# One set of squares, weighted two ways: the double norm behind a feed-forward loop

## The chip, the cores and the metric

One core of one Trainium2 chip runs the whole program. The metric is device microseconds of one execution, median of the runs. TensorE is PE in the rows (PEld its weight loads), VectorE is DVE, ScalarE is ACT, SyncE is SP; GpSimd (POOL) has six instructions and plays no part here.

## The reference, cut to what matters

Two transformer blocks follow each other on 256 tokens of width 1024, all in float32. The first block ends in a feed-forward layer and a final norm; the second begins with a norm of its own and a projection. So two norms stand in a row, with no matmul between them:

```
h = h + _swiglu(_rmsnorm(h, norm_ffn_w), w_gate, w_up, w_down)   # first block
x = _rmsnorm(h, norm_final_w)[:, N_META:]                        # final norm, gain g
...
u = _rmsnorm_2(x, mix_norm_g_2[0])                               # second block, gain m
p = u @ ev_w_in_2                                                # sq, sk, za, sv parts of p
...
x = x + _even_mixer(...)                                         # x itself is needed again
```

With S1 = sum of h² and S2 = sum of (g h)² over the 1024 features, the final norm's factor is rf = 1/sqrt(S1/D + eps), and the second norm's factor on top is 1/sqrt(rf² S2/D + eps). The product of both is 1/sqrt(sum of (g² + eps) h² / D + eps²): one weighted sum, one root, one reciprocal. The factor rf alone is still needed for x, which the residual adds later.

## The kernel before

Tokens lie along the free axis (256 columns), features along the partitions (8 tiles of 128, index k). Every weight matrix streams through in chunks of 2048 columns a partition, in a ring of four slots. SP loads a chunk (`raw`), ACT rounds it (`whi`, L1035), DVE takes the rest (`wlo`, L1409), and PE multiplies with three matmuls a tile (L417: high by high, high by low, low by high). This rounding and subtracting is called splitting a chunk here. A slot's next load waits for the split, and ACT's next rounding in a slot for PE's last use of it.

ACT and DVE split by `pump(n)`, called from their own program: it splits all chunks up to n + 3 that are not split yet, so a chunk's split stands in each engine's queue at a fixed place, behind whatever is written ahead of it. Each engine runs its instructions strictly in the written order; semaphores join them. The order is written out by hand.

PE's projections use `proj`, two pairs of PSUM banks by turns: a projection begins when the chunk is split (`lo_ready`) and when DVE has read out the chunk two before (`proj_free`).

Around the change, in order of the program:

- The feed-forward loop ends. For each of four pairs of feature tiles DVE adds the result to `x_all` (semaphore `x_new`), ACT rounds two tiles to `u` (L1190) and squares the pair (L1191, into region f2), and DVE takes the low part of `u` (L1412, `u_ready`). In the kernel before ACT then squares both tiles again with the final gain as scale (L1196, into f3), and only then posts `sq_ready`.
- PE projects chunk sq0. In its first half a gate ahead of every second tile waits for `u_ready`, and sums the squares of the pair before by matmuls with a matrix of ones (`square_pair`, L474 plain and L479 with the gain).
- ACT takes the root of the plain sum (L1044); DVE makes rf (L1785), turns the second sum into a mean, ACT takes its root (L1254), DVE inverts (L1789) and multiplies: `rms`, the combined factor.
- DVE reads out sq0, sq1, sk0, sk1 with `rms`, and behind sq0 and sq1 scales four tiles each of `x_all` by rf (`x_all` L1412). PE projects sq1, sk0, sk1, turns `rms` into a column for each token (L488), transposes eight small tiles (L811), projects za2, sums squares of q and k for their own norms (L820), projects za3, spreads the factors (L827), projects za0, and the attention begins.

Of the kernel before, what the change touches and what calls it, by code (L numbers as in the profile page):

```python
# [7 lines left out]
ALU = mybir.AluOpType  # L8
ACT = mybir.ActivationFunctionType
# [175 lines left out]
def build(nc, w, params, consts, late, ln_gb, out):  # L185
# [11 lines left out]
    with ExitStack() as ctx:  # L197
# [21 lines left out]
        def C(name):  # L219
            a, n = CONST_COLS[name]  # L220
            return cst[:, a:a + n]
# [43 lines left out]
        both_gains = small[:, 64:72]  # L265

# [140 lines left out]
        def _(pe):  # L407
# [62 lines left out]
            def square_pair(c, norm_no, tokens=S, second=False):  # L470

                pe.wait_ge(sems["sq_ready"], 4 * norm_no + c + 1)
                for k in (2 * c, 2 * c + 1):
                    ins = mm(aux[:, 0, 0:tokens], C("ones"), sq_of(tokens)[:, k, :], start=k == 0, stop=k == KT - 1,  # L474
                             skip_group_check=True)
                if second and c:

                    for k in range(0 if c == 1 else 2 * c, 2 * c + 2):
                        ins = mm(aux[:, 1, 0:S], C("ones"), f("f3", 0, KT, S)[:, k, :], start=k == 0, stop=k == KT - 1,  # L479
                                 skip_group_check=True)  # L480
                if c == 3:
                    ins.then_inc(sems["sumsq"], 1)

# [7 lines left out]
            def sq_of(tokens):  # L491
                return sq if tokens == L else f("f2", 0, KT, S)
# [312 lines left out]
            for name in ("sq1", "sk0", "sk1"):  # L805
                project(name, t0=META, t=S)
            turn_norm(2)
# [216 lines left out]
        def _(eng):  # L1024
# [154 lines left out]
            def norm(source, gain, norm_no, second=False):  # L1179

                for c in range(4):
                    if isinstance(source, str):

                        pump(index[f"{source}{min(c + 1, 3)}"])
                        read_out(f"{source}{c}")
                    else:
                        eng.wait_ge(sems["x_new"], 4 * source + c + 1)
                    pair = x2[:, 2 * c:2 * c + 2, :]
                    for k in (2 * c, 2 * c + 1):
                        A.post(act(u[:, 0, k, META:L], x2[:, k, :], ACT.Copy, scale=gain(k)), "u_hi")  # L1190
                    ins = act(f("f2", 0, KT, S)[:, 2 * c:2 * c + 2, :], pair, ACT.Square)  # L1191
                    if second:
                        A.run(ins)

                        for k in (2 * c, 2 * c + 1):
                            ins = act(f("f3", 0, KT, S)[:, k, :], x2[:, k, :], ACT.Square, scale=V("final", k))  # L1196
                            if k % 2 == 0:
                                A.run(ins)
                    A.post(ins, "sq_ready")
                if not isinstance(source, str):  # L1200

                    pump(loop_last[source] - 1)
                eng.wait_ge(sems["sumsq"], norm_no + 1)
                root(aux[:, 0, 0:S], r_all[:, 0, 0:S], 1.0 / D, eps, "root_ready")
# [46 lines left out]
            norm(0, lambda k: both_gains[:, k:k + 1], 2, second=True)  # L1251

            eng.wait_ge(sems["second_mean"], 1)
            A.post(act(r_all[:, 2, 0:S], r_all[:, 2, 0:S], ACT.Sqrt, bias=eps, scale=1.0 / D), "second_root")  # L1254
# [147 lines left out]
        def _(eng):  # L1402
# [41 lines left out]
            B.run(ve.memset(eps, EPS))  # L1444
            B.run(ve.memset(gn_eps, GN_EPS))
# [39 lines left out]
            for k in range(4, KT):  # L1485
                keep(k)
            B.run(tt(both_gains, par[:, PAR_COLS["final"][0]:PAR_COLS["final"][0] + KT],
                     par[:, PAR_COLS["mix2"][0]:PAR_COLS["mix2"][0] + KT], ALU.mult))
            pump(index["rq0"] - AHEAD + 2)
# [293 lines left out]
            rf, rm = r_all[:, 1, 0:S], r_all[:, 2, 0:S]  # L1783
            eng.wait_ge(sems["root_ready"], 5)
            B.run(ve.reciprocal(rf, rms))  # L1785
            B.run(tt(rm, rf, rf, ALU.mult))
            B.post(tt(rm, rm, aux[:, 1, 0:S], ALU.mult), "second_mean")
            eng.wait_ge(sems["second_root"], 1)
            B.run(ve.reciprocal(rm, rm))  # L1789
            B.post(tt(rms, rf, rm, ALU.mult), "rms_ready")  # L1790
# [4 lines left out]
            for j, name in enumerate(("sq", "sk")):  # L1795
                for c in range(2):
                    b = arrive(f"{name}{c}", urgent=j == c == 0)
                    freed(tt(pre[j][:, 2 * c:2 * c + 2, :], proj[:, b:b + 2, 0:S], bc(rms, 2), ALU.mult))
                    if j == 0:

                        for k in range(4 * c, 4 * c + 4):
                            B.run(stt(x2[:, k, :], x2[:, k, :], V("final", k), rf, ALU.mult, ALU.mult))
# [8 lines left out]
            token_factors(1)  # L1811
            eng.wait_ge(sems["late_in"], 16)
# [8 lines left out]
            B.run(ve.tensor_copy(ident_r, C("ident")))  # L1821
            B.run(ts(mask_r, LC("mask_strict")[:, 0:P], 1.0, ALU.subtract, MASKED, ALU.mult))
            za_part(2)

            B.run(ve.tensor_copy(f("f5", 0, 16, 64)[0:16], C("ident")[0:16, 0:16][:, :, None].to_broadcast([16, 16, 64])))
# [315 lines left out]
```

## Time and profile before

| | |
|---|---|
| median of 3 runs | 1178.59 us (1178.41 to 1178.78) |
| profiled execution, its own time | 1178.25 us |
| its span, first to last instruction | 1176.5 us |
| mean granted TensorE clock | 0.977 |
| PE busy | 1122.0 us (95%), 8656 matmuls |
| DVE busy | 745.9 us (63%), 813 instructions |
| ACT busy | 508.6 us (43%), 506 instructions |
| DMA | 177.63 MB, mean 151 GB/s |

The time stands 1.75 us above the span: start and end of the program lie outside it. A busy PE is the rule here, so the places to read are those at which PE waits. A clock of 1.00 is TensorE's 2.4 GHz level, 0.50 its 1.2 GHz level. One matmul in float32 leaves two entries in the trace, one in the rounded type one.

### The profile page before, as it was taken

Reading aid. Unit: us, or ns where it says so; the run is one execution under the profiler, and the core shown is the slowest. Engines: PE = TensorE matmul, PEld = TensorE weight load, DVE = VectorE, ACT = ScalarE, POOL = GpSimd, SP = SyncE. Lnnn points to the kernel's source line nnn. Section 1 sums busy time; section 2 is a strip of 40 time slices with the busy share of each in tenths; the row PEclk is TensorE's granted clock in tenths of the full one; section 3 lists DMA queues with packets and bytes.
Section 4 is the critical chain, followed back from the end, with each engine's and each line's share of the span. In section 5 each row is a group of like instructions: output and inputs, shape, how many; then the busy total and the mean of one; then the engine's idle time right before and its main releaser. Section 6 shows DMA issues by size and latency. Waiting matters only on the chain.

```text
span 1176.5 us, 21013 instructions
## 1 busy us (share of the span) xinstructions
PE 1122.0 (95%) x8656; PEld 1068.6 (91%) x8656; DVE 745.9 (63%) x813; ACT 508.6 (43%) x506; POOL 6.0 (1%) x6
## 2 busy tenths in 40 slices
PE   8999998899999999998998999999988999999998
PEld 7998885788989999988887999999978999999998
DVE  5764747576756666668746565555479776655563
ACT  5523332433544444455484444333443455434331
POOL 0000001000000000000000000000000000000000
PEclk8999999899999999999999999999898999999999
DMA  9673243134427565664423464654253435564630
GB/s 299 188 211 108 90 143 108 44 130 154 129 72 210 166 203 170 191 201 150 150 95 108 143 215 158 199 177 145 85 165 112 139 108 176 183 211 157 203 107 36
DMA packets 162590, 177.63 MB, mean 151 GB/s; under 512 B 4800, under 2 KB 148288, under 8 KB 162536
## 3 DMA queue, kind: packets, MB, share of 16 engines
q1 hardware_dynamic: 160704, 174.56, 46.9%
q10 hardware_dynamic: 1832, 2.30, 1.0%
q8 instruction: 40, 0.66, 0.2%
q14 instruction: 14, 0.11, 0.0%
HBM read 175.27 MB, written 1.57 MB: 150 GB/s over the span
## 4 chain that ended last, share of the span: by engine, by line
PE 79%; DVE 12%; ACT 5%; issue 2%; DMA 2%; ACTq 0%; SPq 0%; DVEq 0%
PE proj L417 48%; PE aux L778 20%; DVE wlo L1409 4%; DVE f L1412 2%; DVE f L1409 2%; PE aux L474 2%; ACT whi L1035 1%; PE aux L705 1%; DMA gamma_rows<-f 1%; DVE f L1415 1%; PE aux L688 1%; PE aux L585 1%; PE aux L574 1%; DMA f<-in_x_dram 1%; PE aux L698 1%
## 5 line engine op out<-in xcount | busy, mean ns | idle before, releaser
L417 PE MATMUL proj<-u,whi 128*128 128x256 f32 (+1 forms) x2912 | 538.7, 286 | 11.2 <-DVE wlo L1409 4.1
L1409 DVE TENSOR_TENSOR wlo<-raw,whi 128x2048 fp32r<-128x2048 f32 (+2 forms) x176 | 374.2, 2126 | 159.7 <-ACT whi L1035 151.7
L417 PEld LDWEIGHTS proj<-u,whi 128*128 128x128 f32 x2912 | 455.9, 191 | 20.3 <-issue 8.0
L417 PE MATMUL proj<-u,wlo 128*128 128x256 f32 (+1 forms) x1456 | 413.7, 284 | 0.0
L1035 ACT ACTIVATE whi<-raw 128x2048 fp32r<-128x2048 f32 (+3 forms) x174 | 311.6, 1791 | 124.8 <-PE proj L417 56.0
L417 PEld LDWEIGHTS proj<-u,wlo 128*128 128x128 f32 x1456 | 279.0, 192 | 0.0
L778 PE MATMUL aux<-v,whi 128*128 128x256 f32 x1376 | 249.9, 283 | 2.7 <-DVE v L1409 2.5
L778 PEld LDWEIGHTS aux<-v,whi 128*128 128x128 f32 x1376 | 214.2, 192 | 3.4 <-issue 3.4
L778 PE MATMUL aux<-v,wlo 128*128 128x256 f32 x688 | 194.6, 283 | 0.0
L778 PEld LDWEIGHTS aux<-v,wlo 128*128 128x128 f32 x688 | 131.9, 192 | 0.0
L417 PE MATMUL proj<-v,whi 128*128 128x256 f32 (+2 forms) x592 | 109.1, 286 | 6.5 <-DVE f L1409 3.4
L417 PEld LDWEIGHTS proj<-v,whi 128*128 128x128 f32 (+1 forms) x592 | 91.5, 189 | 10.6 <-issue 5.8
L1234 ACT ACTIVATE v<-f 128x512 fp32r<-128x512 f32 x32 | 20.2, 631 | 165.0 <-DVE f L1409 165.0
L417 PE MATMUL proj<-v,wlo 128*128 128x256 f32 (+2 forms) x296 | 83.7, 283 | 0.0
L417 PE MATMUL proj<-whi,u 128*128 128x256 f32 (+1 forms) x352 | 68.9, 290 | 4.1 <-DVE f L1415 2.5
L1409 DVE TENSOR_TENSOR f<-proj,r_all 128x256 f32<-128x256 f32 (+6 forms) x89 | 50.2, 564 | 27.4 <-PE proj L417 23.4
L417 PEld LDWEIGHTS proj<-whi,u 128*128 128x128 f32 x352 | 58.2, 199 | 5.9 <-issue 4.2
L417 PEld LDWEIGHTS proj<-v,wlo 128*128 128x128 f32 (+1 forms) x296 | 55.9, 189 | 0.0
L1409 DVE TENSOR_TENSOR v<-f,v 128x512 fp32r<-128x512 f32 (+1 forms) x54 | 31.5, 584 | 38.0 <-ACT v L1234 24.7
L417 PE MATMUL proj<-wlo,u 128*128 128x256 f32 (+1 forms) x176 | 50.8, 289 | 0.0
L1412 DVE SCALAR_TENSOR_TENSOR f<-proj,r_all 128x512 f32<-128x512 f32 x32 | 22.1, 692 | 44.1 <-PE proj L417 43.5
L1409 DVE TENSOR_TENSOR f<-f 128x512 f32<-128x512 f32 (+5 forms) x63 | 40.7, 646 | 2.2
(263 smaller groups left out, 752.3 us busy)
## 6 DMA issues: line engine op xcount, KB each, us to landing
raw<-in_mlp_w_dram SPq DMA_DIRECT2D x64, 1024.0 KB, 5.3
raw<-in_w_in_dram SPq DMA_DIRECT2D x21, 1024.0 KB, 6.9
raw<-in_od_w_in_dram SPq DMA_DIRECT2D x12, 1024.0 KB, 5.4
raw<-in_w_ffn_gate_dram SPq DMA_DIRECT2D x22, 512.0 KB, 3.9
raw<-in_w_ffn_up_dram SPq DMA_DIRECT2D x22, 512.0 KB, 5.2
raw<-in_w_ffn_down_dram SPq DMA_DIRECT2D x21, 512.0 KB, 5.3
raw<-in_ev_w_in_dram SPq DMA_DIRECT2D x10, 1024.0 KB, 5.6
raw<-in_w_ret_out_dram SPq DMA_DIRECT2D x4, 1024.0 KB, 5.3
```

Of the source, the lines that this page charges most:

```text
L417: ins = mm(o, w_of(a, k), x_of(b, k), start=first and k == 0 and j == 0, stop=last and k == kt - 1 and j == 2, skip_group_check=skip)
L474: ins = mm(aux[:, 0, 0:tokens], C("ones"), sq_of(tokens)[:, k, :], start=k == 0, stop=k == KT - 1, skip_group_check=True)
L574: ins = mm(aux[:, 2 * (h % 2), j * S:(j + 1) * S], k_ret[p0:p0 + 64, h // 2, t:t + P], q_ret[p0:p0 + 64, h // 2, :], start=True, stop=True)
L585: ins = mm(o, rv_tok[:, 1 - j, h * P:(h + 1) * P], sd[:, h % 2, j, :], start=False, stop=j == 1)
L688: ins = mm(aux[:, b, 0:L], q_all[0:96, h, b * P:(b + 1) * P], k_all[0:96, h, :], start=True, stop=True)
L698: ins = nc.tensor.transpose(o, prob[:, h % 2, b, t:t + m], C("ident"))
L705: ins = mm(aux[p0:p0 + 64, 3, S:2 * S], v_tok[0:m, j, 64 * h:64 * h + 64], pt[0:m, j, :], start=j == 0, stop=j == 2)
L778: ins = mm(aux[:, j // 2, (j % 2) * S:(j % 2 + 1) * S], W(a, n, 0, kt, D)[:, q, j * P:(j + 1) * P], v[:, b, 2 * (k % 2) + q, :], start=fir ...
L1035: A.post(act(whi[:, n % RING, 0:wd], raw[:, n % RING, 0:wd], ACT.Copy), "hi_ready")
L1234: A.post(act(v[:, 0, 2 * (k % 2):2 * (k % 2) + 2, :], f("f1", 512, 2, S), ACT.Copy), "hidden_hi")
L1409: return ve.tensor_tensor(o, a, b, op)
L1412: return ve.scalar_tensor_tensor(out=o, in0=a, scalar=s, in1=b, op0=op0, op1=op1)
```

## The change

ACT no longer squares a second time. The one set of squares is summed twice: first with weights g² + eps (a column of eight values for each partition, spread over 128 columns by an address step of zero), inside the gate of sq0, and then with ones, in `first_sums` behind sq0. The first sum gives the combined factor by one root (bias eps²) and one reciprocal; the second gives rf by one root and one reciprocal. The weights are made once near the program's start. The scaling of `x_all` by rf is put behind later read-outs, and three small preparations on DVE (two casts or copies of an identity, one mask) come earlier.

```diff
@@ PE
                 for k in (2 * c, 2 * c + 1):
-                    ins = mm(aux[:, 0, 0:tokens], C("ones"), sq_of(tokens)[:, k, :], start=k == 0, stop=k == KT - 1,
+                    weights = gains_and_eps[:, k:k + 1].to_broadcast([P, P]) if second else C("ones")
+                    ins = mm(aux[:, 0, 0:tokens], weights, sq_of(tokens)[:, k, :], start=k == 0, stop=k == KT - 1,
                              skip_group_check=True)
-                if second and c:
-                    for k in range(0 if c == 1 else 2 * c, 2 * c + 2):
-                        ins = mm(aux[:, 1, 0:S], C("ones"), f("f3", 0, KT, S)[:, k, :], start=k == 0, stop=k == KT - 1,
-                                 skip_group_check=True)
+            def first_sums():
+                for k in range(KT):
+                    ins = mm(aux[:, 1, 0:S], C("ones"), sq_of(S)[:, k, :], start=k == 0, stop=k == KT - 1)
+                ins.then_inc(sems["first_sums"], 1)
...
             project("sq0", t0=META, t=S, gate=by_pair(2, second=True))
-            for name in ("sq1", "sk0", "sk1"):
+            first_sums()
+            project("sq1", t0=META, t=S)
+            turn_norm(2)
+            for name in ("sk0", "sk1"):
                 project(name, t0=META, t=S)
-            turn_norm(2)
@@ ACT
-                    if second:
-                        A.run(ins)
-                        for k in (2 * c, 2 * c + 1):
-                            ins = act(f("f3", 0, KT, S)[:, k, :], x2[:, k, :], ACT.Square, scale=V("final", k))
-                            if k % 2 == 0:
-                                A.run(ins)
...
-            eng.wait_ge(sems["second_mean"], 1)
-            A.post(act(r_all[:, 2, 0:S], r_all[:, 2, 0:S], ACT.Sqrt, bias=eps, scale=1.0 / D), "second_root")
+            eng.wait_ge(sems["first_sums"], 1)
+            root(aux[:, 1, 0:S], r_all[:, 1, 0:S], 1.0 / D, eps, "first_root")
@@ DVE
+            B.run(ve.memset(eps_sq, EPS * EPS))
...
+            B.run(tt(gains_and_eps, final_gains, final_gains, ALU.mult))
+            B.run(ts(gains_and_eps, gains_and_eps, EPS, ALU.add))
...
-            eng.wait_ge(sems["root_ready"], 5)
-            B.run(ve.reciprocal(rf, rms))
-            B.run(tt(rm, rf, rf, ALU.mult))
-            B.post(tt(rm, rm, aux[:, 1, 0:S], ALU.mult), "second_mean")
-            eng.wait_ge(sems["second_root"], 1)
-            B.run(ve.reciprocal(rm, rm))
-            B.post(tt(rms, rf, rm, ALU.mult), "rms_ready")
+            norm_scale(2)
...
+            qk_raw(0, 0, urgent=True)
+            eng.wait_ge(sems["late_in"], 16)
+            B.run(ve.tensor_copy(f("f5", 0, 16, 64)[0:16], C("ident")[0:16, 0:16][:, :, None].to_broadcast([16, 16, 64])))
+            B.run(ve.tensor_copy(ident_r, C("ident")))
+            B.run(ts(mask_r, LC("mask_strict")[:, 0:P], 1.0, ALU.subtract, MASKED, ALU.mult))
+            qk_raw(0, 1)
+            eng.wait_ge(sems["first_root"], 1)
+            B.run(ve.reciprocal(rf, rf))
+            final_scale(0, 2)
+            qk_raw(1, 0)
+            token_factors(1)
+            final_scale(2, 6)
+            qk_raw(1, 1)
...
             za_part(2)
+            final_scale(6, 8)
```

Here `qk_raw(j, c)` is the read-out of sq0, sq1, sk0, sk1 in turn (with the splits that its `arrive` pumps; the first pumps none), and `final_scale` the scaling of `x_all` by rf.

**PE, the gate of sq0.** Names: `aux` is the PSUM tensor of the sums, f2 and f3 the regions of squares, cst the ones, small the new weights. Before, from the second pair of tiles on:

```order
L474 MATMUL aux<-f2,cst 128x256 [waits sq_ready]
L474 MATMUL aux<-f2,cst 128x256
L479 MATMUL aux<-f3,cst 128x256 x4
L417 MATMUL proj<-u,whi 128x256 [waits u_ready]
...
L474 MATMUL aux<-f2,cst 128x256 [waits sq_ready]
L474 MATMUL aux<-f2,cst 128x256
L479 MATMUL aux<-f3,cst 128x256 x2
L474 MATMUL aux<-f2,cst 128x256 [waits sq_ready]
L474 MATMUL aux<-f2,cst 128x256
L479 MATMUL aux<-f3,cst 128x256 x2
```

and after the change, with the place behind sq0:

```order
L476 MATMUL aux<-f2,small 128x256 [waits sq_ready]
L476 MATMUL aux<-f2,small 128x256
L418 MATMUL proj<-u,whi 128x256 [waits u_ready]
...
L476 MATMUL aux<-f2,small 128x256 [waits sq_ready]
L476 MATMUL aux<-f2,small 128x256
L476 MATMUL aux<-f2,small 128x256 [waits sq_ready]
L476 MATMUL aux<-f2,small 128x256
...
L484 MATMUL aux<-f2,cst 128x256 x8
L418 MATMUL proj<-u,whi 128x256 [waits proj_free,lo_ready]
```

The eight matmuls of the second sum have moved from between the gate's waits to a place between sq0 and sq1, and take the plain squares.

**ACT, behind the last squares.** `raw`, `whi` are a chunk's slots; the three roundings are those of sk0, sk1 and za2. Before, then after:

```order
L1035 ACTIVATE whi<-raw 128x2048 [waits chunk_used,raw_landed1,sq_ready]
L1044 ACT_TABLE_LOAD [waits sumsq]
L1044 ACTIVATE r_all<-aux,small 128x256 [waits hi_ready]
L1254 ACTIVATE r_all<-r_all,small 128x256 [waits second_mean,root_ready]
L1035 ACTIVATE whi<-raw 128x2048 [waits chunk_used,raw_landed2,second_root]
```

```order
L1040 ACTIVATE whi<-raw 128x2048 [waits chunk_used,raw_landed1,sq_ready]
L1049 ACT_TABLE_LOAD [waits sumsq]
L1049 ACTIVATE r_all<-aux,small 128x256 [waits hi_ready]
L1049 ACTIVATE r_all<-aux,small 128x256 [waits first_sums,root_ready]
L1040 ACTIVATE whi<-raw 128x2048 [waits chunk_used,raw_landed2,first_root]
```

The second root now waits for PE's `first_sums`, where it waited for DVE's mean, and the rounding of sk0 still stands behind it.

**DVE, from the factor to the read-out of sq1.** Before (the three `wlo` are the splits of sk0, sk1, za2), then after:

```order
L1785 RECIPROCAL r_all<-r_all 128x256 [waits root_ready,lo_ready]
L1409 TENSOR_TENSOR r_all<-r_all 128x256 [waits dve_step]
L1409 TENSOR_TENSOR r_all<-r_all,aux 128x256 [waits dve_step]
L1789 RECIPROCAL r_all<-r_all 128x256 [waits second_root,second_mean]
L1409 TENSOR_TENSOR r_all<-r_all 128x256 [waits dve_step]
L1415 TENSOR_SCALAR small<-par 128x1 [waits rms_ready]
L1409 TENSOR_TENSOR f1<-proj,r_all 128x512 [waits chunk_used,dve_step]
L1412 SCALAR_TENSOR_TENSOR x_all<-x_all,par,r_all 128x256 [waits proj_free]
L1412 SCALAR_TENSOR_TENSOR x_all<-x_all,par,r_all 128x256 [waits dve_step] x3
L1409 TENSOR_TENSOR wlo<-raw,whi 128x2048 [waits hi_ready,dve_step]
L1409 TENSOR_TENSOR wlo<-raw,whi 128x2048 [waits hi_ready,lo_ready] x2
L1409 TENSOR_TENSOR f1<-proj,r_all 128x512 [waits chunk_used,lo_ready]
```

```order
L1717 RECIPROCAL r_all<-r_all 128x256 [waits root_ready,lo_ready]
L1412 TENSOR_SCALAR small<-par 128x1 [waits rms_ready]
L1406 TENSOR_TENSOR f1<-proj,r_all 128x512 [waits chunk_used,dve_step]
L1800 COPY f5<-cst 16x1024 [waits late_in,proj_free]
L1801 CAST v<-cst 128x128 [waits dve_step]
L1412 TENSOR_SCALAR v<-cst 128x128 [waits dve_step]
L1406 TENSOR_TENSOR wlo<-raw,whi 128x2048 [waits hi_ready,dve_step]
L1406 TENSOR_TENSOR wlo<-raw,whi 128x2048 [waits hi_ready,lo_ready] x2
L1406 TENSOR_TENSOR f1<-proj,r_all 128x512 [waits chunk_used,lo_ready]
L1805 RECIPROCAL r_all<-r_all 128x256 [waits first_root,proj_free]
L1409 SCALAR_TENSOR_TENSOR x_all<-x_all,par,r_all 128x256 [waits dve_step] x2
L1406 TENSOR_TENSOR wlo<-raw,whi 128x2048 [waits hi_ready,dve_step]
```

Ahead of the split of sk0 one reciprocal, three products and four scalings are gone, and three small preparations have come; the reciprocal for rf and two scalings now stand behind the read-out of sq1.

## Rows read from the trace of the kernel before

**Rows 1.** The page, chain that ended last: shares of the span by engine.
```profile
PE 79%; DVE 12%; ACT 5%; issue 2%; DMA 2%; ACTq 0%; SPq 0%; DVEq 0%
```
**Rows 2.** The chain in order of time, 505 to 600 us: start, us, what.
```profile
518.55 0.70 DVE x_all L1409
...
519.34 0.52 ACT u L1190
...
520.42 0.64 ACT f L1191
521.08 0.52 ACT f L1196
...
530.65 1.92 ACT whi L1035
...
532.66 2.30 DVE wlo L1409
534.98 1.76 DVE r_all L1785
...
538.36 1.76 DVE r_all L1789
...
541.52 0.50 DVE x_all L1412
...
543.61 2.30 DVE wlo L1409
545.95 13.12 PE proj L417 x96
559.07 0.53 PE aux L488 x4
559.60 1.02 PE aux L811 x8
560.62 5.68 PE proj L417 x48
...
575.75 3.65 PE aux L827 x16
579.39 7.39 PE proj L417 x48
```
**Rows 3.** Groups of ACT's instructions, 519 to 531 us.
```profile
L1196 ACT ACTIVATE f<-x_all,par 128x256 f32<-128x256 f32 x8 | 4.1, 509 | 0.3
```
**Rows 4.** Stretches: length, then busy us of each engine, PEclk, DMA share, GB/s.
```profile
520.40:533.00 12.60, 10.85 (x57) 8.75 (x56) 5.19 (x11) 11.81 (x20) 0.00 (x0) 1.00 0.01 2
...
541.90:545.90 4.00, 0.00 (x0) 0.00 (x0) 3.85 (x5) 2.16 (x2) 0.00 (x0) 1.00 0.00 0
546.10:549.40 3.30, 3.30 (x16) 3.30 (x17) 3.27 (x2) 0.00 (x0) 0.00 (x0) 0.50 0.69 228
...
580.10:583.60 3.50, 3.50 (x19) 3.50 (x18) 3.33 (x6) 1.35 (x2) 0.00 (x0) 0.51 0.00 0
```
**Rows 5.** PE in order of time, the first matmul of sq0 and its restart.
```profile
521.15 0.35 PE L417 MATMUL proj<-u,whi 128*128 128x256 f32 x1 [0.55 <-DVE u L1412]
...
532.31 0.47 PE L417 MATMUL proj<-u,whi 128*128 128x256 f32 x1
```
**Rows 6.** The chain later, two float32 sums (four entries) of a plain norm.
```profile
654.04 0.86 PE aux L474 x4
```
**Rows 7.** Line 670, weight loads with an address step of zero: min/median/max ns.
```profile
L670 PEld LDWEIGHTS aux<-f,cst x16: 180/185/185, 196.3 to 199.5; 8*128 8x128 f32 x16
```
**Rows 8.** ACT in order of time, the squares of q.
```profile
551.36 1.06 ACT L1259 ACTIVATE f<-f 128x1024 f32<-128x1024 f32 x1 [7.27 <-DVE f L1409]
```
**Rows 9.** DVE in order of time, near the program's start and at 567 us.
```profile
20.12 0.17 DVE L1409 TENSOR_TENSOR small<-par 128x8 f32<-128x8 f32 x1
...
23.45 2.29 DVE L1409 TENSOR_TENSOR wlo<-raw,whi 128x2048 fp32r<-128x2048 f32 x1 [0.84 <-ACT whi L1035]
...
567.46 0.68 DVE L1825 COPY f<-cst 16x1024 f32<-16x1024 f32 x1
```

More of the change, by code:

```diff
@@ L265, in build @@
         both_gains = small[:, 64:72]
+        gains_and_eps, eps_sq = small[:, 8:16], small[:, 3:4]
         x_tok = f("f1", 0, 3, D)
@@ L1177, in _, with norm @@
                 A.post(act(v[:, 0, 2 * j:2 * j + 2, :], yr[:, 2 * j:2 * j + 2], ACT.Copy, scale=0.5), "merged_hi")
-            def norm(source, gain, norm_no, second=False):
+            def norm(source, gain, norm_no, eps_ap=eps):
                 for c in range(4):
@@ L1203, in norm @@
                 eng.wait_ge(sems["sumsq"], norm_no + 1)
-                root(aux[:, 0, 0:S], r_all[:, 0, 0:S], 1.0 / D, eps, "root_ready")
+                root(aux[:, 0, 0:S], r_all[:, 0, 0:S], 1.0 / D, eps_ap, "root_ready")
             def hidden_layer(d):
@@ L1250, in _ @@
             hidden_layer(FFN)
-            norm(0, lambda k: both_gains[:, k:k + 1], 2, second=True)
-            eng.wait_ge(sems["second_mean"], 1)
-            A.post(act(r_all[:, 2, 0:S], r_all[:, 2, 0:S], ACT.Sqrt, bias=eps, scale=1.0 / D), "second_root")
+            norm(0, lambda k: both_gains[:, k:k + 1], 2, eps_ap=eps_sq)
+            eng.wait_ge(sems["first_sums"], 1)
+            root(aux[:, 1, 0:S], r_all[:, 1, 0:S], 1.0 / D, eps, "first_root")
             for j, name in enumerate(("sq", "sk")):
@@ L1488, in _ @@
                      par[:, PAR_COLS["mix2"][0]:PAR_COLS["mix2"][0] + KT], ALU.mult))
+            final_gains = par[:, PAR_COLS["final"][0]:PAR_COLS["final"][0] + KT]
+            B.run(tt(gains_and_eps, final_gains, final_gains, ALU.mult))
+            B.run(ts(gains_and_eps, gains_and_eps, EPS, ALU.add))
             pump(index["rq0"] - AHEAD + 2)
@@ L1780, in _ @@
             hidden_layer(FFN, 0, lambda k: both_gains[:, k:k + 1], 2)
-            rf, rm = r_all[:, 1, 0:S], r_all[:, 2, 0:S]
-            eng.wait_ge(sems["root_ready"], 5)
-            B.run(ve.reciprocal(rf, rms))
-            B.run(tt(rm, rf, rf, ALU.mult))
-            B.post(tt(rm, rm, aux[:, 1, 0:S], ALU.mult), "second_mean")
-            eng.wait_ge(sems["second_root"], 1)
-            B.run(ve.reciprocal(rm, rm))
-            B.post(tt(rms, rf, rm, ALU.mult), "rms_ready")
+            rf = r_all[:, 1, 0:S]
+            norm_scale(2)
             pre = (f("f1", 0, 4, S), f("f1", 1024, 4, S))
@@ L1794, in _, with qk_raw, final_scale @@
             B.run(ts(qg8, V("sb_q"), 0.125, ALU.mult))
[L1795 to L1802, printed above, removed]
+            def qk_raw(j, c, urgent=False):
+                b = arrive(f"{'sq' if j == 0 else 'sk'}{c}", urgent=urgent)
+                freed(tt(pre[j][:, 2 * c:2 * c + 2, :], proj[:, b:b + 2, 0:S], bc(rms, 2), ALU.mult))
+            def final_scale(k0, k1):
+                for k in range(k0, k1):
+                    B.run(stt(x2[:, k, :], x2[:, k, :], V("final", k), rf, ALU.mult, ALU.mult))
+            qk_raw(0, 0, urgent=True)
[11 more added lines that the diff above has]
+            qk_raw(1, 1)
             def per_token(name, dst, width=256):
@@ L1809, in per_token @@
                 freed(ins)
-            token_factors(1)
-            eng.wait_ge(sems["late_in"], 16)
             eng.wait_ge(sems["sg_turned"], 1)
@@ L1819, in za_part @@
                 per_token(f"za{a}", lambda j: za[:, j, a * 256:(a + 1) * 256])
-            B.run(ve.tensor_copy(ident_r, C("ident")))
-            B.run(ts(mask_r, LC("mask_strict")[:, 0:P], 1.0, ALU.subtract, MASKED, ALU.mult))
             za_part(2)
-            B.run(ve.tensor_copy(f("f5", 0, 16, 64)[0:16], C("ident")[0:16, 0:16][:, :, None].to_broadcast([16, 16, 64])))
+            final_scale(6, 8)
             eng.wait_ge(sems["sb_root"], 1)
```

## The prediction, made before the changed kernel ran

> **What bounds the kernel now.** I read the chain that ended last first: PE holds 79% of the span, DVE 12%, ACT 5% [rows 1]. So the time is PE's row of work plus the places where PE waits, and the change can only pay at such a place. The chain in order of time shows one between 518 and 560 us [rows 2]: it leaves PE for ACT at 519.34 and stays with ACT, over four pairs of tiles, until 530.65, goes through ACT's rounding and DVE's split of sq1, then through DVE's reciprocals, its scaling of `x_all` and the split of sk0, and comes back to PE at 545.95. The second squares stand in it: eight instructions of 256 columns, 509 ns each, 4.1 us in all [rows 3]. The stretches show what PE did meanwhile: busy 10.85 of 12.60 us in the gate, nothing at all from 541.90 to 545.90, and then 3.30 us of work at a granted clock of 0.50, the 1.2 GHz level [rows 4].
>
> **The change on PE's row, step by step.** I count from sq0's first matmul (521.15) to the eight transposes L811 (559.60), which is 38.45 us [rows 2, 5].
>
> *The gate.* From 521.15 to sq0's restart at 532.31 are 11.16 us [rows 5]. The work in it is 18 matmuls of the rounded type at 0.118 (5.68 us for 48 [rows 2]), 2.1 us, and 16 float32 sums, 32 entries at 0.215 (0.86 for four [rows 6]), 6.9 us: 9.0, so PE waited 2.15. After the change a pair costs ACT two roundings and one square, 519.34 to 521.08, or 1.74 us [rows 2], so the four pairs last until 526.3 where they lasted until 530.65. DVE's pace per pair, one addition of 0.70 and two low parts of about 0.5 (bounded by the 0.50 of a scaling with the same 256 columns [rows 2]), is about 1.75 with gaps: the two engines run level, and DVE cannot make it worse by more than about 0.1. The last two sums, 0.86, follow the last square, so sq0 restarts at about 527.25. That is 6.1 us for 2.1 + 3.45 of work: waits of 0.55. **Gain 1.6.** The other eight sums, 3.45 us, are not saved: they move behind sq0.
>
> *The wait for sk0.* Before, PE stands idle 4.05 us (541.90 to 545.95 [rows 2, 4]) for the split of sk0, which stands on DVE behind two reciprocals of 1.76, three products, and four scalings of 0.50 [rows 2]. After: sq0 ends 30 matmuls (3.55) after 527.25, at 530.8, the first sums at 534.25 (call it T). The root waits there, ACT needs about 0.5 for it (256 columns, as its rounding of 0.52) and 1.92 for sk0, DVE 2.30 for the split [rows 2]: with 0.3 for handing over, sk0 is split at T + 5.1. PE meanwhile does sq1 (5.7) and L488 (0.53), until T + 6.2. The idle time is gone, with 1.1 us to spare. **Gain 4.05.**
>
> *The half-rate stretch.* sk0 and sk1 took 13.12 us where 96 matmuls at full clock take 2 x 5.68 = 11.36 [rows 2]; the clock fell as PE's idle time ended [rows 4]. Without the idle time there is no reason for it. **Gain 1.75.**
>
> Here a rule of the Trainium skill speaks against the change. In this case's rows the gate, 12.60 us with 1.75 of it idle in several short pieces, ran at 1.00 throughout [rows 4], so shorter waits in it should cost nothing. TensorE: Matmul & The Clock Gate, section "A second HAM failure mode: psum-queue depth-cycling", says that frequent short idle times between groups of matmuls make the clock swing between its two levels. If it held in the new gate, one stretch at half rate would come back, priced like the old one, and the sum would be 5.65 in place of 7.4. The trace disagrees for the old gate, which had more waiting in it, so I keep the row's answer.
>
> *Costs.* The weights with an address step of zero: the trace has such loads, 8 partitions by 128 columns, at 185 ns [rows 7]; a load below the 0.215 us between entries lies beside the matmuls. I take nothing for them; the bound below is nothing (a shorter load is hidden as well), the bound above is in the rivals. The setup on DVE, a product of 8 columns (0.17 [rows 9]) and an addition of the same size, about 0.4 with gaps, and a memset that is smaller still, stands ahead of a split that waited 0.84 for ACT behind it [rows 9]: nothing. Without that cover it would be 0.4. The three preparations on DVE, 0.68 [rows 9] and two of 128 columns that I bound by 0.5 each, at most 1.7, run between the read-out of sq0 (about 533.3) and the rounding of sk0 (T + 2.7 = 537.0), where DVE has 3.7 us to wait. Without that cover they would cost up to 1.7 less the 1.1 to spare.
>
> *What is late next.* All of ACT's and DVE's work up to the attention's norms hangs on T too, so I put both queues beside PE's, in us after T, with 2.30 a split, 1.92 a rounding, 0.70 a read-out (as the addition of 512 columns), 1.76 a reciprocal, 0.50 a scaling [rows 2]. PE wants sk0 at 6.2, sk1 at 11.9, za2 at 18.6 (after L811's 1.02), L820 at 24.3. DVE ends the splits of sk1 and za2 at 9.7 and reads out sq1 at 10.4, which frees sk1's banks: 1.5 to spare. The reciprocal for rf, two scalings, the split of za3 and the read-out of sk0 end at 16.5: 2.1 to spare for za2. Four scalings, the split of za0 and the read-out of sk1 end at 21.9, ACT's squares (1.06 [rows 8]) at 23.0: 1.3 to spare for L820. So nothing overtakes PE, but no cover is above 2.1. From L827 on (575.75 before) everything in the chain is released by PE and moves with it.
>
> **Sum.** 1.6 + 4.05 + 1.75 = 7.4 us. The profiled execution's 1178.25 (span 1176.5 plus 1.75 outside) becomes 1170.85; the median of the runs lies 0.34 higher, so 1171.2.
>
> **Rivals.**
>
> *The clock gives back more (chance 0.15).* At 580.10 to 583.60 PE ran at 0.51 with no idle time ahead of it, right behind L827's 3.65 us of small matmuls; za0 took 7.39 instead of 5.68 [rows 2, 4]. That stretch is not tied to a wait of PE. If it does not come back at its new place, 1.7 more is gained: 1169.5. Against it: the four times of the kernel before lie within 0.53 us, so its half-rate stretches hardly wander. By the Trainium skill, TensorE: Matmul & The Clock Gate, Part 1, the monitor runs free of the kernel's start, so where a stretch falls may change from run to run; by that rule the times would scatter by such amounts. No run here shows that they do.
>
> *A wait takes the old one's place (0.20).* ACT now stands at `first_sums` with the roundings of sk0, sk1, za2 behind it, and DVE's splits behind those. If these queues are slower than I add up, by more than the 1.1 to 1.5 us of cover, PE waits again at sk0, at sk1 or at L820. Each us beyond costs one; an idle time as long as the old one would bring the half-rate stretch with it. With 1 to 2.5 us late, and the stretch (1.75) or not, the gain is 3 to 6.4: 1172.2 to 1175.6. For it: four covers must hold at once. Against: they come from measured durations and all start at one point.
>
> *The gain is taken back later (0.05).* If the attention after 586 us were held by something that does not move with PE, the time would be about 1178. Against: the chain enters it through PE [rows 2].
>
> *Slow weights (0.05, slower in 0.03).* The sixteen loads of 128 partitions with a step of zero have no row; the nearest has 8 partitions [rows 7]. Beyond 0.215 us each costs its excess. The whole gain of 7.4 is gone at 0.215 + 7.4/16 = 0.68 us a load, 3.7 times the row; at 1.0 us the cost is 12.6 and the time 1183.8. Against: a step of zero took no longer than a common load there.
>
> **How the numbers follow.** My forecast has 0.55, with a range of its own of 1170.0 to 1172.2 (0.2 for DVE's pace and setup, 0.7 for handing over, both ways). The predicted time is its 1171.2. The range for 8 in 10 reaches down to the first rival less its spread, 1168.9, and up through most of the second, 1174.5. About 0.2%, 2.4 us, is what a measurement of this kernel can tell from no change. Faster by more: 0.55 + 0.15 + 0.20 = 0.90. Within: 0.05 + 0.02 = 0.07. Slower: 0.03.
>
> **What would show it right or wrong.** ACT's four pairs end near 526.3 and `first_sums` near 534.3. PE shows no idle time over 1 us between 527 and 560 and a clock of 1.00 there. L811 begins near 552.2 and L827 near 568.3. The new sums' entries stand 0.215 apart; if they are further apart, the weights are slow. If PE waits before sk0, sk1 or L820, the row ahead of it names the cover that failed. If L811 comes at 552 and the end still does not move by 7, the chain behind 586 us was wrong.

## The result, and the profile after

| | before | changed |
|---|---|---|
| median us (runs) | 1178.59 (7: 1173.00 to 1179.25) | 1168.09 (7: 1167.41 to 1169.47) |
| profiled execution: time, span us | 1178.25, 1176.5 | 1167.41, 1165.6 |
| mean granted clock | 0.977 | 0.978 |
| PE busy | 1122.0 us, 95% | 1118.1 us, 96% |

The ratio is 0.9921 [0.9907, 0.9935]: the change is worth 9.3 us of 1178.59 (7.7 to 11.0). The forecast of 1171.2 had the sign; its gain of 7.4 us falls 1.9 short of that. The median lies 3.1 us below the forecast and 0.8 us below the lower end of the range; the ratio times 1178.59, 1169.3, lies within it.

The page's shares of the chain that ended last have moved from DVE to PE, against [rows 1]:

```profile
PE 80%; DVE 10%; ACT 5%; issue 2%; DMA 2%; ACTq 0%; SPq 0%; DVEq 0%
```

The chain of the changed kernel in order of time (start, us, what) answers to [rows 2]. L476 are the weighted sums in the gate, L484 `first_sums`, L491 the turning of the factor, L816 the eight transposes, L825 the sums of q and k, L832 the spreads (L827 before), L845 the first scores.

```profile
520.08 0.94 PE proj L418 x6
521.02 0.86 PE aux L476 x4
521.88 0.84 PE proj L418 x6
...
524.48 1.92 PE aux L476 x8
526.40 3.51 PE proj L418 x30
529.92 3.46 PE aux L484 x16
533.37 5.64 PE proj L418 x48
539.01 0.53 PE aux L491 x4
539.54 11.56 PE proj L418 x96
551.10 0.88 PE aux L816 x8
...
557.65 3.56 PE aux L825 x16
...
567.08 3.65 PE aux L832 x16
570.73 5.88 PE proj L418 x48
576.61 0.64 PE aux L845 x4
```

From 520.08 to 576.61 the chain stays with PE: in the chain before it left for ACT at 519.34 and came back at 545.95. The gate takes 6.32 us (520.08 to 526.40), sq1 follows `first_sums` at once, and 96 matmuls of sk0 and sk1 take 11.56 where they took 13.12. From sq0's first matmul to the transposes are 31.02 us, 38.45 before: **7.43 less**. Below I give this stretch by the starts in PE's own order of time, which go a little differently about the transposes: 38.38 before, 30.86 after, 7.52 less.

The same engine by stretches (length, then busy us of PE, weight loads, DVE, ACT, POOL, then PEclk, DMA share, GB/s) answers to [rows 4]. PE is busy for the whole gate, and where it stood still from 541.90 on it now runs at 1.00. Behind the spreads no half rate shows either: za0's 48 matmuls take 5.88 in the chain above, where they took 7.39.

```profile
520.40:533.00 12.60, 12.60 (x80) 11.01 (x79) 9.42 (x13) 8.24 (x12) 0.00 (x0) 1.00 0.18 59
533.00:541.90 8.90, 8.90 (x74) 8.73 (x73) 6.29 (x5) 6.22 (x4) 0.00 (x0) 1.00 0.38 126
541.90:552.00 10.10, 10.10 (x88) 10.10 (x87) 9.37 (x12) 4.90 (x3) 0.00 (x0) 1.00 0.90 283
```

ACT and DVE in order of time (start, us, instruction, in brackets the idle time ahead of it and who ended it):

```profile
525.25 1.91 ACT L1040 ACTIVATE whi<-raw 128x2048 fp32r<-128x2048 f32 x1
...
533.47 0.47 ACT L1049 ACTIVATE r_all<-aux,small 128x256 f32<-128x256 f32 x1 [4.52 <-PE aux L484]
...
536.00 6.94 DVE L1406 TENSOR_TENSOR wlo<-raw,whi 128x2048 fp32r<-128x2048 f32 x3 [2.50 <-ACT whi L1040]
542.98 0.69 DVE L1406 TENSOR_TENSOR f<-proj,r_all 128x512 f32<-128x512 f32 x1
...
549.20 0.69 DVE L1406 TENSOR_TENSOR f<-proj,r_all 128x512 f32<-128x512 f32 x1
...
554.52 0.69 DVE L1406 TENSOR_TENSOR f<-proj,r_all 128x512 f32<-128x512 f32 x1
555.31 1.06 ACT L1256 ACTIVATE f<-f 128x1024 f32<-128x1024 f32 x1 [6.58 <-DVE f L1406]
```

ACT ends its pairs at 525.22, does the rounding of sq1 and the first root, and then waits 4.52 us for `first_sums`; DVE's split of sk0 is the first of the three at 536.00 and ends at 536.00 + 2.30 = 538.3, while PE wants it at 539.54. So the wait has changed sides: ACT and DVE wait for PE.

### The profile page after: what moved, and what is told of

It reads as the page before. It is cut to its first block, busy times and chain, and to the rows that moved or that the text cites. A ratio compares the mean times of both kernels' runs of the same rounds, so it can differ in the third digit from the quotient of the medians.

```text
span 1165.6 us, 21006 instructions
## 1 busy us (share of the span) xinstructions
PE 1118.1 (96%) x8656; PEld 1063.9 (91%) x8656; DVE 745.0 (64%) x813; ACT 504.6 (43%) x498; POOL 6.0 (1%) x6
## 4 chain that ended last, share of the span: by engine, by line
PE 80%; DVE 10%; ACT 5%; issue 2%; DMA 2%; ACTq 0%; SPq 0%; DVEq 0%
PE proj L418 49%; PE aux L781 20%; DVE wlo L1406 4%; DVE f L1409 2%; DVE f L1406 2%; PE aux L476 2%; ACT whi L1040 1%; PE aux L708 1%; DMA gamma_rows<-f 1%; PE aux L691 1%; DVE f L1412 1%; PE aux L588 1%; PE aux L577 1%; PE aux L701 1%; DMA f<-in_x_dram 0%
## 5 line engine op out<-in xcount | busy, mean ns | idle before, releaser
L418 PE MATMUL proj<-whi,u 128*128 128x256 f32 (+1 forms) x352 | 66.4, 284 | 4.0 <-DVE f L1412 2.5
```

Source lines behind the costliest of these rows:

```text
L418: ins = mm(o, w_of(a, k), x_of(b, k), start=first and k == 0 and j == 0, stop=last and k == kt - 1 and j == 2, skip_group_check=skip)
```

## The experiments

The theory to be tested: PE's row is the bound, and the gain is the second squares (gate, and the chain to sk0 behind it), the idle time ahead of sk0, and the half-rate stretch that this idle time brought. The rival: other edits (the order of the scalings, the place of the sums) or only the clock did it. "Stretch" is from sq0's first matmul to the first transpose in the profile; "spreads to scores" is from L827 or L832 to the first scores, 9.5 us where PE has the full clock and 11.0 with one half-rate stretch. Both columns are of the one profiled execution of a run. Times are medians of all its executions; each ratio is against the kernel before, run beside it (its medians there: 1177.39, 1176.26, 1176.90).

| run | median us | ratio | stretch | spreads to scores |
|---|---|---|---|---|
| before (first profile) | 1178.59 | 1 | 38.38 | 11.04 |
| changed (first profile) | 1168.09 | 0.9921 [0.9907, 0.9935] | 30.86 | 9.53 |
| e1_squares_back | 1172.90 | 0.9968 [0.9955, 0.9982] | 35.18 | 11.03 |
| e2_scalings_only | 1172.49 | 0.9967 [0.9956, 0.9978] | 36.31 | 9.52 |
| e3_norm_only | 1169.83 | 0.9943 [0.9927, 0.9959] | 31.64 | 11.04 |
| e4_pe_filled | 1176.23 | 0.9995 [0.9982, 1.0008] | 36.87 | 12.62 |
| e5_sums_in_gate | 1166.60 | 0.9925 [0.9901, 0.9950] | 30.51 | 9.53 |
| e6_rounded_sums | 1165.74 | 0.9911 [0.9892, 0.9930] | 27.70 | 9.52 |
| after_again (the changed kernel) | 1168.65 | 0.9931 [0.9908, 0.9953] | 30.93 | 9.52 |
| before_again (the kernel before) | 1176.65 | 1.0002 [0.9987, 1.0016] | 38.37 | 11.03 |
| e7_rounded_in_gate | 1165.22 | 0.9906 [0.9888, 0.9924] | 27.39 | 12.63 |
| after_third | 1168.40 | 0.9940 [0.9920, 0.9959] | 30.91 | 9.52 |
| before_third | 1176.78 | 1.0005 [0.9988, 1.0022] | 38.42 | 11.02 |

**The second squares back on ACT.** The changed kernel, but ACT squares each pair a second time; nobody reads these squares.

```diff
                     ins = act(f("f2", 0, KT, S)[:, 2 * c:2 * c + 2, :], pair, ACT.Square)
+                    if second:
+                        A.run(ins)
+                        for k in (2 * c, 2 * c + 1):
+                            ins = act(f("f3", 0, KT, S)[:, k, :], x2[:, k, :], ACT.Square, scale=V("final", k))
...
                     A.post(ins, "sq_ready")
```

> The changed kernel, with ACT's eight second squares put back ahead of each sq_ready (written to their old region, read by nobody). The measure is the stretch from sq0's first matmul to the first of the eight transposes: 38.45 us before, 31.02 in the changed kernel. Theory (three waits of PE: the gate 1.6, the wait for sk0 4.05, the half-rate stretch 1.75): ACT's four pairs last 4.3 us longer, PE waits for them in the gate, sq0 restarts some 10.3 us after its first matmul in place of 6.3, and nothing else changes, since all later queues start at the end of the first sums: stretch 35.0, some 4 us above the changed kernel. Rival (the squares were hidden, the gain is DVE's shorter path to the split of sk0): stretch 31 to 31.5.

The chain of this kernel:

```profile
528.62 0.52 ACT f L1200
...
530.31 3.51 PE proj L418 x30
...
543.45 11.56 PE proj L418 x96
...
570.99 3.79 PE aux L832 x16
574.78 7.24 PE proj L418 x48
```

ACT paces the gate again: sq0 restarts 10.64 us after its first matmul (519.67) instead of 6.32, and all the rest of the stretch is as in the changed kernel, down to the 11.56 of sk0 and sk1. The squares cost 35.18 - 30.86 = 4.3 us, eight times 0.54, as the theory had it. The gate as a stretch:

```profile
519.70:531.00 11.30, 8.07 (x42) 5.99 (x43) 4.14 (x8) 10.75 (x18) 0.00 (x0) 1.00 0.00 1
```

PE waits 3.2 us of it, in several pieces, at 1.00. But the half-rate stretch behind the spreads is there (7.24 for za0's 48 matmuls), although the sums and the norm are the new ones.

**The order of the scalings alone.** The kernel before, with its two sets of squares and its norm; only the scaling of `x_all` stands where the change puts it.

```diff
...
+            qk_raw(0, 0, urgent=True)
+            qk_raw(0, 1)
+            final_scale(0, 2)
+            qk_raw(1, 0)
+            final_scale(2, 6)
+            qk_raw(1, 1)
...
             za_part(2)
-
+            final_scale(6, 8)
```

> The kernel before, with one part of the change: the scalings of x_all by rf are moved behind later read-outs, none is left ahead of the split of sk0. Norm, squares and sums stay as before. Theory: the split of sk0 comes four scalings, 2.05 us, earlier, so PE's idle time of 4.07 us shrinks to about 2.0; if that is too short for the clock to fall, the half-rate stretch goes too: measured stretch 38.45 - 2.05 - 1.75 = 34.65; if the clock still falls, 36.4. Rival (the moved scalings matter little, the norm's own path is all): stretch 38 or more.

PE in order of time at sk0, and a stretch of the same kernel:

```profile
541.98 0.50 PE L417 MATMUL proj<-u,whi 128*128 128x256 f32 x2 [1.98 <-DVE wlo L1409]
```

```profile
543.20:546.50 3.30, 3.30 (x17) 3.30 (x17) 3.27 (x2) 0.00 (x0) 0.00 (x0) 0.50 1.00 339
```

The idle time at sk0 is 1.98 in place of 4.05, so the stretch is 2.07 shorter: four scalings of 0.50. The clock fell all the same, as PE's work came back: half the idle time saved only itself. Without the half-rate stretch 34.65 was expected. Behind the spreads this kernel, with the old norm, shows none. Its time fell by more than the stretch, 2.6 to 5.2 us for 2.07: as in the changed kernel, part of what was gained lies outside the stretch.

**The norm alone.** The changed kernel with the scalings, the three preparations and the factors at the places where the kernel before has them.

```diff
             qk_raw(0, 0, urgent=True)
...
             eng.wait_ge(sems["first_root"], 1)
             B.run(ve.reciprocal(rf, rf))
-            final_scale(0, 2)
+            final_scale(0, 4)
+            qk_raw(0, 1)
+            final_scale(4, 8)
             qk_raw(1, 0)
...
```

> The changed kernel with the other part undone: the scalings of x_all are back behind the read-outs of sq0 and sq1, four and four, and the three preparations back at their old places; the norm with one set of squares stays. Theory: DVE does the reciprocal for rf and four scalings, 3.9 us, before the split of sk0, starting when the first root is there (0.8 us behind the end of the first sums), so that split ends about 7.0 us behind them where PE wants it at 6.2: PE waits some 0.8 us, stretch 31.8, and the clock stays at 1.00. Rival (the order on DVE is worth a large part of the gain): stretch 33 or more.

The chain of this kernel at sk0,

```profile
538.59 2.30 DVE wlo L1406
...
540.93 11.61 PE proj L418 x96
```

and PE in order of time at the same place:

```profile
540.93 0.50 PE L418 MATMUL proj<-u,whi 128*128 128x256 f32 x2 [0.69 <-DVE wlo L1406]
```

The reciprocal and four scalings stand ahead of the split again, the cover of 1.1 us is used up, and PE waits 0.69 for it; the clock stayed up (11.61). So the order is worth 0.8 us (31.64 - 30.86) on top of the norm and 2.07 without it: the norm carries 6.7 of the 7.5. The two do not add up, because both take away from the one wait.

**PE filled.** The kernel before with 32 unused matmuls between sq1 and sk0, so that PE has work while it waits.

```diff
-            for name in ("sq1", "sk0", "sk1"):
+            project("sq1", t0=META, t=S)
+            for j in range(32):
+                mm(aux[:, 3, 0:S], u[:, 0, j % KT, META:META + P], u[:, 1, j % KT, META:L], start=True, stop=True)
+            for name in ("sk0", "sk1"):
...
```

> The kernel before with 32 more matmuls on PE behind sq1, into a bank that nobody reads, of the rounded type with 256 columns: 32 x 0.118 = 3.8 us of work in the place of the 4.07 us in which PE stood idle for the split of sk0. All waits stay. Theory (idle time alone makes the clock fall there): sk0 and sk1 take about 11.4 us in place of 13.12, the stretch shrinks by 1.75 to 36.7 though PE does more. Rival (the clock falls there for another reason): sk0 and sk1 still take about 13, stretch 38.4.

PE in order of time, and the chain of this kernel:

```profile
539.73 3.95 PE L807 MATMUL aux<-u 128*128 128x256 f32 x32
543.94 0.51 PE L417 MATMUL proj<-u,whi 128*128 128x256 f32 x2 [0.26 <-DVE wlo L1412]
```

```profile
543.94 11.62 PE proj L417 x96
...
572.23 4.85 PE aux L830 x16
577.09 7.77 PE proj L417 x48
```

sk0 begins as late as ever, but sk0 and sk1 take 11.62 instead of 13.12: the idle time did bring the half rate, and it cost 1.5 us. The time does not show it: the ratio's interval, 0.9982 to 1.0008, holds 1.5 us as well as nothing. In the profiled execution the last two rows say where it went: the half-rate stretch behind the spreads is twice as long, 12.62 us from spreads to scores where the kernel before has 11.04. There the clock took back 30 us later what it had given at sk0.

**The plain sums inside the gate.** The changed kernel with the matmuls of `first_sums` behind each pair's weighted sums, where the kernel before had its second sums.

```diff
+                if second and c:
+                    for k in range(0 if c == 1 else 2 * c, 2 * c + 2):
+                        ins = mm(aux[:, 1, 0:S], C("ones"), sq_of(S)[:, k, :], start=k == 0, stop=k == KT - 1,
...
-            first_sums()
             project("sq1", t0=META, t=S)
```

> The changed kernel, with the first sums (plain ones, same squares) put back into the gate of sq0, behind the weighted sums of each pair as before the change. In the changed kernel the stretch from sq0's first matmul to the transposes is 30.9 us. Theory (PE's own work is all that is left in that stretch): it makes no difference where in it PE does its 3.45 us; a pair's sums and matmuls in the gate are 2.4 us for PE against 1.74 for ACT, so PE no longer waits there, but the factor comes 3.4 us later, which nobody waits for: stretch 30.6 to 31.1. Rival (taking the sums out of the gate was worth something by itself): stretch 32 or more.

The chain of this kernel:

```profile
519.00 0.95 PE proj L418 x6
...
528.38 9.19 PE proj L418 x78
```

The stretch is 30.51, 0.35 shorter and 0.1 below the expected range: with all sixteen sums in the gate sq0 restarts after 9.38 us (519.00 to 528.38), where the changed kernel needs 6.32 and then 3.46. So the sums fill part of the small gaps that ACT's pairs leave. Moving the eight sums behind sq0 was therefore not where the gain came from, as the theory says. The times tell nothing apart here (1166.60 and 1168.65 beside each other, intervals that overlap).

**Rounded sums.** The changed kernel with squares and weights rounded to the type of the projections' operands before they are summed; the sums are a little less exact for it.

```diff
+        rounded = sb("rounded", [P, KT + 1], F32R)
...
-                    weights = gains_and_eps[:, k:k + 1].to_broadcast([P, P]) if second else C("ones")
+                    weights = gains_r[:, k:k + 1].to_broadcast([P, P]) if second else C("ones")
+                    squares = v[:, k // 4, 2 * (k % 4) + 1, :] if second else sq_of(tokens)[:, k, :]
```

> The changed kernel with both sums in the rounded type: ACT writes the squares rounded, the weights and a column of ones are rounded too, and a sum of 256 columns is one pass of 0.118 us in place of two of 0.215. The sums are a little less exact. Theory (PE bounds the stretch, one to one): the first sums take 0.95 in place of 3.46, the gate ends 0.85 earlier behind ACT's last square, all queues have some 0.4 us to spare: stretch 27.5 in place of 30.9, the time 3.3 us below the changed kernel. Rival (DVE's and ACT's queues become the bound, since their work is unchanged): stretch 29 or more, with PE waiting at sk0, sk1 or at the sums for q and k.

The chain of this kernel:

```profile
525.85 3.54 PE proj L420 x30
529.38 0.91 PE aux L487 x8
```

`first_sums` shrink from 3.46 to 0.91 and the gate from 6.32 to 5.70 (from 520.15), together 3.2, and the stretch is 3.16 shorter. So the 2.55 saved in `first_sums` count one to one. The gate's own eight sums shrink as much, but only 0.62 of that comes through, 0.85 was expected: there ACT's four pairs are the pace again. The median was 1165.74 beside 1168.65 of the changed kernel; the single times overlap (1163.97 to 1168.46 and 1167.12 to 1169.15).

**Rounded sums inside the gate.** The last two edits together.

> The kernel with rounded sums, with the first sums moved into the gate of sq0 too. With rounded sums the stretch from sq0's first matmul to the transposes is 27.7 us, and PE now waits in the gate for ACT and DVE again (1.6 us). Theory (a sum is free where PE waits anyway, and costs its length where PE does not): of the 0.91 us of the first sums all but the last pair's 0.24 disappear in the gate's waits: stretch 27.0, or up to 27.2 if the split of sk0, which then has nothing to spare, holds PE up a little. Rival (DVE's queue, unchanged, becomes the bound at sk0): 27.6 or more.

The chain of this kernel:

```profile
528.16 2.30 DVE wlo L1408
...
530.51 5.91 PE proj L420 x48
```

The stretch is 27.39, 0.3 shorter than with the sums behind sq0 and not 0.5 to 0.7: sq1 now begins when DVE has split it, a wait of 0.2 to 0.3 us that I had not listed. With 1165.22 this has the lowest median, not told apart from the 1165.74 of the rounded sums alone, and 3.2 below the changed kernel beside it (1168.40); its runs, 1164.14 to 1168.19, lie below all of that one's, 1168.30 to 1172.14. Its profile has a half-rate stretch of twice the usual length behind the spreads (12.63 us to the scores).

**Both kernels again.** The changed kernel and the one before, twice more each with a profile, to see which of the places come back.

> The changed kernel once more, for a second profile. Theory (the gain beyond 7.4 us is half-rate stretches and a start that wander from run to run): the stretch is 30.9 again, but the half-rate stretches outside it need not stand where they stood; behind the spreads of the factors one may come, which makes 11.0 us of the 9.5 from there to the first scores. Rival (the change itself removes that half-rate stretch): 9.5 again.

> The kernel before once more, for a second profile. Theory (wandering): stretch 38.4 again with PE idle for 4.07 us and a half-rate stretch behind it, while the 11.0 us from the spreads to the first scores may be 9.5 this time. Rival (that half-rate stretch belongs to the kernel before): 11.0 again.

> The changed kernel a third time, for the half-rate stretch behind the spreads of the factors, which both profiles of it lacked and both profiles of the kernel before had. If the change removes it: 9.5 us from the spreads to the first scores again. If it falls by where the spreads happen to lie: 11.0 is as possible as 9.5. The stretch from sq0's first matmul to the transposes stays at 30.9 either way.

> The kernel before a third time, for the same question. If that half-rate stretch belongs to the kernel before: 11.0 us from the spreads to the first scores. If it falls by chance: 9.5 is possible. The stretch from sq0's first matmul to the transposes stays at 38.4.

The chain behind the spreads, first of before_third, then of after_third:

```profile
578.04 7.38 PE proj L417 x48
```

```profile
571.65 5.88 PE proj L418 x48
```

All three profiles of the kernel before have the half-rate stretch behind the spreads, none of the three of the changed kernel has it. The three pairs account for the profiled times, each line worked out from the starts (sq0's first matmul came at 521.15, 520.71 and 519.76 before, at 520.08, 520.87 and 520.96 after):

| us less after the change | first pair | "again" | "third" |
|---|---|---|---|
| start of sq0 | 1.07 | -0.16 | -1.20 |
| stretch, sq0 to transposes | 7.52 | 7.44 | 7.51 |
| spreads to scores | 1.51 | 1.51 | 1.50 |
| PE's restart after a wait, 614 to 630 us | -1.15 | -1.00 | -1.26 |
| everything else | 1.89 | 1.84 | 1.22 |
| profiled time | 10.84 | 9.63 | 7.77 |

The stretch repeats within 0.1 us. The start of sq0 does not belong to the change: it goes either way from run to run.

The fourth row is a loss. Some 38 us behind the scores PE waits 5.49 us for DVE, and a half-rate stretch follows in all the kernels. PE in order of time, from that restart to the next projection, in the first profile before and the first after:

```profile
624.66 1.94 PE L897 MATMUL proj<-cst,f 128*128 128x128 f32 x8 [5.49 <-DVE f L1412]
...
630.03 0.50 PE L417 MATMUL proj<-v,whi 128*128 128x256 f32 x2
```

```profile
614.50 1.94 PE L902 MATMUL proj<-cst,f 128*128 128x128 f32 x8 [5.49 <-DVE f L1409]
...
621.02 0.50 PE L418 MATMUL proj<-v,whi 128*128 128x256 f32 x2
```

and the same two kernels as a stretch (before, then after):

```profile
600.00:640.00 40.00, 34.51 (x271) 31.67 (x271) 20.05 (x25) 24.50 (x24) 0.00 (x0) 0.96 0.32 105
600.00:640.00 40.00, 34.51 (x262) 31.83 (x261) 21.47 (x26) 23.21 (x23) 0.00 (x0) 0.91 0.27 89
```

The same work takes 5.37 us before and 6.52 after. So of the 1.5 us that the changed kernel no longer loses behind the spreads, it loses 1.0 to 1.3 here, in all three pairs. The other kernels do the same: the three that have a half rate behind the spreads and 5.2 to 5.4 us here are the norm alone, the filled PE and the rounded sums in the gate; the three that have none there and 6.5 to 6.6 here are the scalings alone, the sums in the gate and the rounded sums. Only the kernel with the squares back has both (11.03 and 6.53). The rest, "everything else", lies almost wholly behind 830 us: from 640 to 830 PE is busy for 189.9 of 190 us at 1.00 in both kernels. What it is was not traced.

## Why the prediction was right, and where it was wrong

*The gate: right.* Predicted a restart after 6.1 us and a gain of 1.6. The 11.16 us before were read in PE's own order of time; read in the same way, the changed kernel has

```profile
526.05 0.59 PE L418 MATMUL proj<-u,whi 128*128 128x256 f32 x2
...
529.75 3.62 PE L484 MATMUL aux<-f,cst 128*128 128x256 f32 x16
533.02 0.58 PE L418 MATMUL proj<-u,whi 128*128 128x256 f32 x2
```

so sq0 restarts 5.97 us after its first matmul (520.08), the first sums take 3.27, and the gain is 11.16 - 5.97 - 3.27 = 1.9. The 6.32 of the chain cannot be set against 11.16. ACT's pairs ended 5.14 us after sq0's first matmul, predicted 5.15 (526.3 for 521.15).

*The wait for sk0: right.* The 4.05 us are gone. The split ends 4.9 us after the first sums (T = 533.37), predicted 5.1; PE wants it 6.2 after them. Norm alone, without the new order, had 0.69 of it left.

*The half-rate stretch: right.* 13.12 became 11.56, 1.56 against 1.75: the term took 11.36 for the 96 matmuls at full clock, 0.2 too little. That it hung on the idle time is shown by the filled PE (11.62) and by the order alone, where 1.98 us of idle time still brought it. All four profiles with 1.98 us or more of it ahead of sk0 have the half rate, and none of the nine with 0.69 or less.

*The rule weighed.* The row's answer held: the new gate ran at 1.00, and so did the one with 3.2 us of waits in pieces. TensorE: Matmul & The Clock Gate, section "A second HAM failure mode: psum-queue depth-cycling", of the Trainium skill would have the clock swing under frequent short waits; no run here shows that, and the gain of 5.65 that went with it is refuted.

*Costs: right.* The weights with a step of zero load as fast as the full ones. By the source view of line 476 (kind, names and count, then ns min/median/max, first and last start, shapes):

```profile
L476 PEld LDWEIGHTS aux<-f,cst x80: 186/190/192, 21.4 to 977.8; 128*128 128x128 f32 x80
...
L476 PEld LDWEIGHTS aux<-f,small x16: 185/188/191, 520.7 to 525.8; 128*128 128x128 f32 x16
```

*What is late next: right.* The end of each piece of work, in us after T, predicted and measured: read-out of sq1 10.4 and 10.3, of sk0 16.5 and 16.5, of sk1 21.9 and 21.8, ACT's squares 23.0 and 23.0, and PE wants them at 24.3. The rival of a wait in the old one's place is refuted: nothing overtook PE.

*The sum: right for its stretch.* 7.4 predicted, 7.4 to 7.5 measured in three pairs of profiles. Its terms are off by 0.3 us and less, the gate too low and the half rate too high, so part of the closeness is luck. All of the 7.5 reaches the end of the program (7.8 to 10.8 us of profiled time), so it was not taken back later. For what the time gained beyond it the sum had no term.

*What failed: the first rival.* The step was "the four times of the kernel before lie within 0.53 us, so its half-rate stretches hardly wander". Later runs of the same kernel lie between 1172.46 and 1180.28 (and one at 1181.32, with a granted clock of only 0.926), with medians near 1176.9. The record lists the mean granted clock of each, and the times go with it: 15 runs at 0.973 average 1178.98 us, 25 at 0.977 average 1176.26, 7 at 0.980 average 1174.42. Four times were too few to say that the clock hardly wanders, and the 0.15 for a clock that gives more back rested on them. The rival's condition came true in all three profiles of the changed kernel: behind the spreads 1.5 us (1.7 predicted) did not come back. Its price did not, since 1.0 to 1.3 of that was lost again behind the next long wait. So that its 1169.5 lies next to the 1169.3 of the ratio is luck.

*What stays open.* Where the time beyond 7.5 us comes from, and whether it belongs to the change. In the profiles it is 3.3, 2.2 and 0.3 us: the start of sq0, the half-rate stretches behind the spreads and behind the wait after them, and what lies behind 830 us, 1.2 to 1.9, untraced. The half rate behind the spreads is not the norm's: three kernels with the new one (squares back, norm alone, rounded in the gate) have it, one with the old norm (the scalings alone) has none. Nor does the start of the spreads decide it plainly: at 570.99 it is there, at 571.79 it is not, at 572.23 it is twice as long. Over all runs the intervals of the changed kernel's three ratios are 7.7 to 11.0, 5.5 to 10.8 and 4.8 to 9.4 us; the first lies just above 7.5, the other two hold it, and all three hold 9.0.

## What to carry to other kernels

Add up the waits on the row of the engine that bounds the stretch, then put the other engines' queues beside it from one common point: here five such queue times came out within 0.2 us, and the sum within 0.15. Where one norm's sums can be weighted on TensorE, the squares need to be made once. Where the second sum stands mattered little: in the gate it was 0.35 us cheaper than behind it. Before a range is drawn, look for half-rate stretches that no wait explains, and give their coming and going more than one profile's weight: here one was worth a fifth as much as the change itself.

## What the hardware showed that was not expected

The clock fell behind only 1.98 us of idle time (0.50 for 3.3 us in the scalings' run), but not behind 0.69 us in the norm's, nor behind the pieces in any gate.

A half-rate stretch also came with no idle time at all, behind 3.65 us of the spreads' small matmuls: not at all, once or twice as long (9.5, 11.0 or 12.6 us from spreads to scores), alike in the three profiles of each of the two kernels, and different in kernels that differ by less than 1 us in where the spreads begin. By TensorE: Matmul & The Clock Gate, Part 1, of the Trainium skill the monitor runs free of the kernel's start. The runs fit this: the times of one kernel scatter from 1172.46 to 1180.28 us and go with the mean granted clock (0.981 to 0.973), while its stretch repeats within 0.1 in three profiles. At which places the clock wanders was not shown run by run.

A saving at one place can be taken back by the clock at another: in its profile the filled PE saved 1.5 us at sk0 and lost 1.6 behind the spreads, and the changed kernel saved 1.5 behind the spreads and lost 1.0 to 1.3 behind the next long wait.
